# Hybrid decoder layer: retention's scores, states and first output moved between the attention's units

## The reference

```python
proj = rms_norm(x, norm1_g) @ w_in               # 3072 columns
dq, dk, dv, rq, rk, rv, rg = split(proj)
# 4 heads of differential attention (q, k: 2 x 64, v: 128), causal, rotary:
a = softmax(q1 k1^T) - lam * softmax(q2 k2^T);  d_out = rms_norm(a @ v) * (1 - lam_init)
# 4 heads of retention (q, k: 64, v: 128), in 4 chunks of 128 tokens, rotary:
scores  = (q k^T) * intra_decay                   # inside a chunk
y_intra = scores @ v
kv      = (k * k_decay)^T v;  state = chunk_decay * state + kv      # from chunk to chunk
y_cross = (q * q_decay) @ state_before
r_out   = rms_norm(y_intra + y_cross) * silu(rg)
x = x + concat(d_out, r_out) @ w_o
x = x + moe(rms_norm(x))                          # 32 experts, top 4
out = rms_norm(x, norm_f_g)
```

## Time and profile before

| | |
|---|---|
| median of 3 runs | 1485.09 us (1483.62 to 1487.18) |
| the profiled execution | 1489.09 us |
| its span in the trace | 1487.4 us |
| PE busy | 1438.4 us, 97% |
| DVE busy | 1280.3 us, 86% |
| ACT busy | 1016.8 us, 68% |
| POOL busy | 233.7 us, 16% |
| weight traffic | 471.98 MB, mean 317 GB/s |

### The profile page before, as it was taken

The page is one execution under the profiler, slowest core; times in us unless marked ns, Lnnn a source line. Parts: engine busy times, 40 slices in busy tenths (PEclk is TensorE's granted clock), DMA queues, the critical chain, the costliest instruction groups (busy, mean ns, idle before and its releaser), DMA issues.

```text
span 1487.4 us, 21906 instructions
## 1 busy us (share of the span) xinstructions
PE 1438.4 (97%) x6777; PEld 1181.7 (79%) x6777; DVE 1280.3 (86%) x1125; ACT 1016.8 (68%) x874; POOL 233.7 (16%) x238
## 2 busy tenths in 40 slices
PE   7999899599999999999999999999999999999996
PEld 6888578478888888888888888888888888888884
DVE  5465847699999999999999999999999999999997
ACT  5424724367777777777777777777777777777774
POOL 0100301411111111111111111211111111121112
PEclk9999989799999999999999999999999999999998
DMA  9442100799999999999999999999999999999994
GB/s 341 181 176 115 44 0 37 243 333 355 366 368 368 364 371 364 378 365 371 374 367 366 386 349 368 380 372 368 365 372 372 366 369 365 377 367 369 370 370 162
DMA packets 131534, 471.98 MB, mean 317 GB/s; under 512 B 15380, under 2 KB 15672, under 8 KB 131320
## 3 DMA queue, kind: packets, MB, share of 16 engines
q1 hardware_dynamic: 118016, 450.94, 80.8%
q0 software_dynamic: 13168, 20.16, 5.5%
q10 hardware_dynamic: 328, 0.60, 0.1%
HBM read 467.96 MB, written 32.51 MB: 336 GB/s over the span
## 4 chain that ended last, share of the span: by engine, by line
PE 91%; DVE 4%; issue 2%; DMA 1%; ACT 1%; POOL 0%; POOLq 0%; DVEq 0%; SPq 0%; ACTq 0%
PE pair L979 24%; PE pair L981 23%; PE pair L987 23%; PE pair L700 3%; PE pair L701 3%; PE pair L705 3%; PE pair L1005 2%; PE pair L993 2%; PE pair L955 2%; PE pair L839 1%; PE pair L840 1%; PE pair L852 1%; DVE split L1806 1%; DMA expert_sums<-work,list_cur 1%; PE pair L792 0%
## 5 line engine op out<-in xcount | busy, mean ns | idle before, releaser
L1806 DVE TENSOR_TENSOR split<-ring,split 128x2048 fp32r<-128x2048 f32 x396 | 892.0, 2288 | 74.3 <-ACT split L1288 74.3
L1288 ACT CAST split<-ring 128x2048 fp32r<-128x2048 f32 x396 | 758.4, 1916 | 201.2 <-PE pair L987 192.1
L979 PE MATMUL pair<-split,operands 128*128 128x512 f32 x1584 | 630.5, 398 | 0.0
L981 PE MATMUL pair<-split,operands 128*128 128x512 f32 x1584 | 618.5, 390 | 0.0
L987 PE MATMUL pair<-split,operands 128*128 128x512 f32 x1584 | 424.4, 390 | 0.0
L987 PEld LDWEIGHTS pair<-split,operands 128*128 128x128 f32 x1584 | 297.3, 188 | 63.2
L979 PEld LDWEIGHTS pair<-split,operands 128*128 128x128 f32 x1584 | 298.1, 188 | 58.8
L981 PEld LDWEIGHTS pair<-split,operands 128*128 128x128 f32 x1584 | 298.2, 188 | 58.6
L2045 POOL DMA_INDIRECT expert_sums<-work,list_cur x32 | 61.1, 1910 | 470.2 <-PE pair L987 438.8
L2038 POOL DMA_INDIRECT work<-h_rows,token_next x35 | 70.3, 2009 | 190.3 <-DMA token_next<-slot_lists 156.6
L1294 ACT CAST operands<-pair 128x512 fp32r<-128x512 f32 x66 | 38.7, 588 | 68.3 <-PE pair L987 41.4
(11 more groups left out here) (258 smaller groups left out, 1144.4 us busy)
## 6 DMA issues: line engine op xcount, KB each, us to landing
ring<-in_w_moe_in SPq DMA_DIRECT2D x264, 1024.0 KB, 9.1
ring<-in_w_moe_out SPq DMA_DIRECT2D x132, 1024.0 KB, 10.5
ring<-in_w_in SPq DMA_DIRECT2D x12, 1024.0 KB, 10.5
ring<-in_w_o SPq DMA_DIRECT2D x4, 1024.0 KB, 10.3
resid<-in_x SPq DMA_DIRECT2D x4, 512.0 KB, 5.4
expert_sums<-zero_rows SPq DMA_DIRECT2D x4, 512.0 KB, 11.7
work<-expert_sums SPq DMA_DIRECT2D x4, 512.0 KB, 5.4
out<-ring SPq DMA_DIRECT2D x4, 512.0 KB, 2.6
```

The costliest lines, as they stand in the source:

```text
L979: pe.matmul(dst[:, f, :], left_hi[:, k0 + k, :], hi[c.buffer][:, k, cols], start=(start and k == 0), stop=False)
L981: pe.matmul(dst[:, f, :], left_lo[:, k0 + k, :], hi[c.buffer][:, k, cols], start=False, stop=False)
L1288: act.copy(hi[c.buffer], raw[c.slot]).then_inc(hi_made, 1)
L1806: dve.tensor_tensor(lo[c.buffer], raw[c.slot], hi[c.buffer].bitcast(F32), ALU.subtract).then_inc(lo_made, 1)
```

## The change

- The keys-and-values products go into PE's step 4, the four score groups into steps 6, 8, 10 and 12, `ret_output(0)` into step 15. All but the output are made in pair 2 (banks 4 and 5), one after the other.
- To free pair 2, the turned maps use bank 6 alone (before: banks 4 and 5 by turns), and the value products bank 7. A transpose now waits for the copy of the unit before it, not of the one before that.
- DVE: the decayed queries go into step 2, the states into step 4, the decays into steps 6, 8, 10 and 12; `gate(0)` goes ahead of the attention's factor and `att_norm(0)`. The end of `gate` that reports a row tile as ready is a helper of its own, `mixed`.
- ACT: the squares of the first output come in step 16, before the last map's copy, and its root behind that copy; the dummy root is gone. In the other chunks the root follows the squares as before.
- The decayed scores and queries move in SBUF to places that are free during the loop.

```diff
-        st_s = w(18432, NT * 512).rearrange(...)
+        st_s = [slot(RAW + 4 + i // 2) ... for i in range(NT)]
-        qdT = w(20480, 2 * SEQ).rearrange(...)
+        qdT = slot(RAW + 1) ... [:, 6 * P:6 * P + 2 * SEQ].rearrange(...)
@@ PE, att_transposes and att_values
-                if u >= 2:
-                    pe.wait_ge(attT_ready, u - 1)
+                if u >= 1:
+                    pe.wait_ge(attT_ready, u)
                 for j in range(i + 1):
-                    mm = pe.transpose(bank[4 + u % 2][:, j * P:(j + 1) * P],
+                    mm = pe.transpose(bank[6][:, j * P:(j + 1) * P],
...
-                    mm = pe.matmul(bank[6][:, h * P:(h + 1) * P], attT[:, u % 2, j * P:(j + 1) * P],
+                    mm = pe.matmul(bank[7][:, h * P:(h + 1) * P], attT[:, u % 2, j * P:(j + 1) * P],
@@ PE, retention (bodies as before, but in pair[2])
+            def ret_score(i):
+                if i == 0:
+                    pe.wait_ge(state_ready, 2 * (NT - 1))
+                else:
+                    pe.wait_ge(ret_decayed, i)
...
             def ret_output(i):
-                pe.wait_ge(ret_decayed, (2, 3, 3, 4)[i])
+                pe.wait_ge(ret_decayed, NT)
@@ PE, the loop, behind att_values(s - 3)
+                if s == 4:
+                    ret_kvs()
+                if s in (6, 8, 10, 12):
+                    ret_score(s // 2 - 3)
+                if s == 15:
+                    ret_output(0)
 
             pe.wait_ge(exp_done, 2 * NU)
             pe.wait_ge(attT_ready, NU)
             pe.wait_ge(av_evicted, NT)
-            ret_kvs()
-            for i in range(NT):
-                ret_score(i)
-            ret_output(0)
             ret_output(1)
@@ ACT
             for s in range(1, NU + 2):
                 if 2 <= s < NU:
                     exponentials(s)
                 if s == NU:
-                    act.activation(stat[:, 55:56], eps_col[:, 0:1], ACT.Sqrt).then_inc(root_table, 1)
+                    ret_squares(0)
                 if s - 1 < NU:
                     turned_map(s - 1)
+                if s == NU:
+                    ret_roots(0)
                 if s >= 5 and (s - 5) % NH == 0:
                     att_rows((s - 5) // NH)
...
-            ret_squares(0)
             ret_squares(1)
+            ret_roots(1)
             mix_evict(0)
@@ DVE
+            def decayed_queries():
+                dve.wait_ge(qk_by_act, 6)
+                dve.wait_ge(qk_by_dve, 6)
...
             for s in range(NU + 1):
                 if 2 <= s < NU:
                     maxima(s)
                 if s >= 1:
                     difference(s - 1)
                 if s >= 7 and (s - 7) % NH == 0:
                     sum_squares((s - 7) // NH)
+                if s == 2:
+                    decayed_queries()
+                if s == 4:
+                    states()
+                if s in (6, 8, 10, 12):
+                    decay(s // 2 - 3)
...
-            decay(0)
-            decay(1)
-            states()
-            decay(2)
-            decay(3)
+            dve.wait_ge(silu_done, NT)
+            gate(0)
             dve.wait_ge(av_evicted, NT)
             dve.wait_ge(att_root, 1)
...
             att_norm(0)
-            gate(0)
+            mixed(0)
             att_norm(1)
```

More of the change, by code:

```diff
@@ new lines, in ret_score @@
+            def ret_score(i):
[3 more added lines that the diff above has]
+                    pe.wait_ge(ret_decayed, i)
+                for h in range(NH):
+                    rows = slice(64 * (h % 2), 64 * (h % 2) + 64)
+                    mm = pe.matmul(pair[2][:, h % 2, (h // 2) * P:(h // 2 + 1) * P],
+                                   qkT[rows, RK_AT + h // 2, i * P:(i + 1) * P],
+                                   qkT[rows, RQ_AT + h // 2, i * P:(i + 1) * P], start=True, stop=True)
+                mm.then_inc(ret_scores, 1)
@@ new lines, in ret_output @@
+            def ret_output(i):
+                pe.wait_ge(ret_decayed, NT)
+                if i >= 1:
+                    pe.wait_ge(state_ready, 2 * i)
+                    pe.wait_ge(qd_ready, 2)
+                if i >= 2:
+                    pe.wait_ge(ret_gated, i - 1)
+                for h in range(NH):
+                    rows = slice(64 * (h % 2), 64 * (h % 2) + 64)
+                    dst = pair[ret_out_at[i]][:, h % 2, (h // 2) * P:(h // 2 + 1) * P]
+                    if i >= 1:
+                        pe.matmul(dst, qdT[rows, h // 2, i * P:(i + 1) * P], state[rows, i - 1, h // 2, :],
+                                  start=True, stop=False)
+                    mm = pe.matmul(dst, st_s[i][:, h % 2, h // 2, :],
+                                   proj[:, i, CRV + h * P:CRV + (h + 1) * P], start=(i == 0), stop=True)
+                mm.then_inc(ret_out, 1)
@@ L1207, in att_rows, with ret_squares, ret_roots @@
                 act.wait_ge(av_evicted, i + 1)
+                if i == NT - 1:
+                    chain.settle()
                 act.activation(square_tmp, mix[:, i, 0:512].rearrange("p (h c) -> p h c", h=NH), ACT.Square)\
                     .then_inc(att_squared, 1)
+            def ret_squares(i):
+                act.wait_ge(squares_summed, NT - 1 if i == 0 else NT)
+                act.wait_ge(ret_out, i + 1)
+                outputs = pair[(2, 3, 2, 3)[i]][:, :, 0:256].rearrange("p r (a c) -> p a r c", a=2)
+                head_squares([outputs[:, h // 2, h % 2, :] for h in range(NH)], i, NH)
+            def ret_roots(i):
+                chain.settle()
+                root(16 + 2 * NH * i + NH, NH, P, ret_root)
             for s in range(1, NU + 2):
@@ L1585, in gate @@
                 dve.sem_inc(mix_ready, 1)
-            decay(0)
-            decay(1)
-            states()
-            decay(2)
-            decay(3)
+            NU = NT * NH
+            for s in range(NU + 1):
+                if 2 <= s < NU:
+                    maxima(s)
+                if s >= 1:
+                    difference(s - 1)
+                if s >= 7 and (s - 7) % NH == 0:
+                    sum_squares((s - 7) // NH)
+                if s == 2:
[4 more added lines that the diff above has]
+                    decay(s // 2 - 3)
+            sum_squares(NT - 1)
+            dve.wait_ge(squares_summed, NT)
+            for n in range(2):
+                chain.settle()
+                ins = dve.tensor_tensor(head_stat[:, :, 0:NH], head_stat[:, :, 0:NH], row_rec[:, :, :], ALU.mult)
+                if n == 0:
+                    chain(ins)
+            ins.then_inc(squares_scaled, 1)
+            dve.wait_ge(silu_done, NT)
+            gate(0)
             dve.wait_ge(av_evicted, NT)
```

103 lines of the change are left out of this document (29 added, 74 removed).

## The result

| | before | after |
|---|---|---|
| median of 6 runs | 1485.07 us (1483.62 to 1487.18) | 1491.03 us (1488.48 to 1491.38) |
| the profiled execution | 1489.09 us | 1491.18 us |
| its span | 1487.4 us | 1489.5 us |
| its mean granted clock | 0.986 | 0.982 |

The changed kernel is slower: its time is 1.0035 of the time before (95% interval 1.0025 to 1.0046), 5.2 us by this ratio and 6.0 by the medians. Forecast were 1484.9 us and at most 1488.4.

What follows compares the result with a forecast made beforehand. VectorE's queue, full in loop and tail, was taken as the bound. Loop +5.1, tail -5.3 and clock 0 net -0.2 us: 1488.9 from the profiled 1489.09, 1484.9 against the 4.0 lower median; range 1481.3 to 1488.4.

Steps and rivals of the forecast that it cites:

- The accounting: Loop growth and tail saving summed, net -0.2 us; given 60%, with 1.5 us of error to each side.
- Loop, +5.1: Attention loop: VectorE's moved queries, states and decays, partly filling its waits, make it 5.1 us longer.
- The new wait: Loop step 4: VectorE's states wait about 0.65 us for TensorE's 24 key and value products.
- The wait behind step 10: Loop: decays in steps 6 and 10 fill VectorE's following waits of 0.70 and 0.44 us, adding only 0.1 and 0.2.
- Tail, -5.3: From the last value product to the first load of the mix transposes: 5.3 us shorter than the old 10.7.
- Single bank, 0: Loop: transposes wait for the previous unit's copy with turned maps in one bank; costs nothing, at most one copy's end.
- First output in step 15, 0: Loop step 15: eight products, 0.5 to 1 us, run while TensorE waits for VectorE; costs nothing.
- the clock's: Tail: the granted clock falls as before, somewhat earlier, at the same cost; taken as 0, bounds -4.2 to +1.5 us.
- Rival (b): Clock falls inside the loop, steps 2 to 6; key and value products take 3 us: 1488 to 1490 us, 14%.
- Rival (c): Loop: each decayed-query product on VectorE waits for one POOL key scaling, 2.0 us more: 1486.9 us, 8%.
- Rival (d): Loop: every VectorE wait is filled, so it grows by only 3.5 us: 1483.3 us, 8%.
- Rival (a): Tail: the clock stays high and the mix begins at full rate, 4.2 us less: 1480.7 us, 10%.

Runs made afterwards that it cites:

- experiment 6: The changed kernel with four unread TensorE products in the idle gap between the last value products and the second retention output: median 1485.03 us, ratio 0.9997.
- experiment 1: The kernel before, run again without any edit for a second profile: median 1485.07 us, ratio 1.0001; the profiled execution took 1484.78 us.
- experiment 3: The changed kernel with eight unread TensorE products in the tail, four in the gap and one before each head of the second retention output: median 1485.73 us, ratio 1.0001.
- experiment 10: The kernel before with only the banks changed, turned maps in bank 6 alone and values in bank 7: median 1485.09 us, ratio 0.9998.
- experiment 7: The changed kernel with four unread TensorE products, one before each head of the second retention output, none in the gap: median 1488.31 us, ratio 1.0021.
- experiment 4: The changed kernel with four unread TensorE products before the transposes of step 4 in the loop: median 1489.66 us, ratio 1.0036.
- experiment 12: The changed kernel with the states in VectorE's step 5 instead of step 4: median 1490.07 us, ratio 1.0036.
- experiment 2: The changed kernel with the decayed queries moved from step 2 to behind the loop, before the last sum of squares: median 1486.08 us, ratio 1.0002.

## Why the prediction was wrong

**The accounting held.** *Loop, +5.1.* From the last projection product to the end of the last values: 188.56 - 151.2 = 37.4 before; 193.03 - 151.2 = 41.8 in experiment 6, at full clock: +4.5. With the fall in the loop it was 195.47 - 152.6 = 42.9: +5.5. The new wait was 0.71 at full clock, forecast 0.65. The wait behind step 10 is gone, as said; that behind step 6, forecast to be gone too, is 0.25. Not foreseen was a wait of 0.45 for the scores of the last unit (at 188.21). *Tail, -5.3:* measured 5.2 long, against 10.7 in the profile before, but the fall already stretched that one by 0.3: in experiment 1 it is 200.43 - 190.08 = 10.4, so -5.2. Net at full clock, by the interval: 58.6 (experiments 3 and 6) - 59.3 (experiment 1) = -0.7, forecast -0.2. *Single bank, 0:* shown by experiment 10. *First output in step 15, 0:* its products ran while PE had nothing to do, and ScalarE's last copy and the table load came in the order laid out; the eviction began 0.3 us behind the last values' end, at 195.77.

**The step that failed is the clock's: "So I expect the same fall, somewhat earlier, and the same cost ... I take 0."** The fall came from about 200.8 to 211.0 us, as the mix transposes began and not somewhat earlier (48.2 us behind the last projection product, before 47.2), and its cost was nearly that of the fall before: 4.6 us behind the first load of the mix (16.1 us from there to `mix_low` against 11.6 in experiment 6), 4.5 in the interval of before. But 0 is right only against an execution that has the fall too. Just before I had written: "The median of the runs shown is 4.0 lower, so the forecast against it is 1484.9." I took those 4 us for scatter that both kernels share. They were the fall: experiment 1 has the same program without it, 4.3 us faster and with an interval 4.5 shorter. By time and mean clock the kernel before falls in 10 executions of 100, the changed one in all six. So against the median of before the term was not 0 but +5.6: 4.6 for the fall in the tail and 1.0 for the one in the loop (by the profile of experiment 6). With the -0.7 of the placement this makes the 4.9 by which the interval of the changed kernel, 64.2, exceeds that of experiment 1. By my own sum an execution with the fall takes 1488.9, and that would have been the forecast, had I asked why the profiled execution was slower than all three runs shown. The rest to the profiled 1491.2 is the 1.4 us by which its projection ended later, 0.6 in the interval (+0.4 for the forecast's -0.2, the loop's fall is in it) and 0.3 behind it.

**Why it now falls each time.** The theory on record, that less dense work is left ahead of the second output, is what experiments 3, 6 and 7 test from its other side: dense products put back into the gap hold the clock in ten of twelve executions and the loss is gone. It is not a matter of one chip: experiments 4 and 12 leave the tail as the change made it, and their 18 executions, on two chips, all lie at 0.982 to 0.984. The 1.08 us of idling ahead of the output seem to matter more than its thin products, though ten of twelve against six of twelve is not much to go by. That the 56 retention products were what held it before is argued from this, not shown: they were not put back by themselves.

**Rival (b), the fall inside the loop, 14%, happened,** in the place named and by its mechanism: the 24 products took 2.83 us (named: 3). It was too dear: 3 to 4 us were named, and the interval shows 0.8 (against experiment 4) to 1.0 (the loop against experiment 6's). The low clock lasted 3.4 us, not 10. And it comes in one of four profiles of this loop. So the time landed near this rival's 1488 to 1490, for the most part for another reason.

**Rival (c), VectorE and POOL.** The two products for the queries took 1.49 instead of 1.28, the four scalings 4.41 instead of 3.90. With the queries elsewhere (experiment 2) the scalings took 3.90 again. So the two products together lost 0.2, not the 2 x 0.98 that (c) charged, and POOL, which has slack, bears the larger part, 0.5. The rule of the Trainium skill (SBUF — State Buffer, Who interferes with whom), that such a pair exclude each other for a whole instruction, is right in that both engines lose time; as a bill of a whole scaling for each product it was too high here.

**Rival (d), more fits than counted,** explains the -0.7: at full clock the loop grew by 4.5 and not 5.1. Half a microsecond is probably a quotient that had stood at 0.69 us beside a POOL operation; in experiment 6 each quotient of these steps takes 0.22.

**Rival (a), the clock stays high, 10%,** did not happen to this kernel; it is what experiments 3 and 6 made by hand. Even then the time is that of the kernel before, 1485, and not 1480.7, because the median of before had the high clock already.

What stays open: why the tail seems to fall in every run of experiments 4 and 12 while the queries' place alone (experiment 2) saves half of them, and what in an execution decides, as the same program goes both ways.

## What to carry to other kernels

Ask first whether the profiled execution is a typical one: if it lies several us off the median, find the stretch that differs (here the granted clock of one tail) before subtracting the difference, because a change can turn the rare case into the rule. Work on TensorE that seems only to be in the way may be what keeps its clock; when it is moved out of a thin stretch, put unread products where it idles, and price the change at both clocks. When a queue is full in two stretches, look for the place where it idles behind them: queries and states belonged into VectorE's 4 us of waiting behind the loop, not between the units.

## What the hardware showed that was not expected

The granted clock is not a function of the program. The same kernel, with PE busy 0.93 of 2 us at the same point and the same instructions around it, dropped to 1.2 GHz in one execution and stayed at 2.4 GHz in another, 4.5 us apart in the interval; in 100 executions ten seem to have fallen, 4 to 6 us above the median. Nor is the place of the fall fixed. In four profiles PE idles the same 1.1 us behind the last value products, and the clock falls 5.3 us behind their end in the changed kernel, 3.5 in experiment 4, 3.1 in experiment 7 and 2.9 in experiment 12; in experiment 2, with the same idling, it does not fall. The profile of experiment 7 also shows that denser work behind the gap does not always undo it:

```profile
194.00:196.00 2.00, 0.96 (x4) 0.62 (x5) 0.42 (x1) 1.46 (x4) 0.00 (x0) 1.00 0.00 0
196.00:198.00 2.00, 2.00 (x8) 1.21 (x8) 1.90 (x9) 0.31 (x1) 0.00 (x0) 0.76 0.00 0
```

while experiment 6, whose gap ahead of the output is filled, idles later and keeps the clock:

```profile
196.00:198.00 2.00, 1.36 (x7) 0.89 (x6) 1.93 (x7) 0.64 (x6) 0.00 (x0) 1.00 0.00 0
```

The mean granted clock of a run sorts the executions only roughly (0.982 to 0.985 mostly with the fall, 0.986 to 0.989 without, but the profiled one of before had it at 0.986); the row of the tail is the proof.
